# Two mixer sections of a transformer kernel: another order of matmul groups, filter taps and norms

## The reference, cut to what matters

```python
h = rmsnorm(x) ; p = h @ w_in            # 256 x N_IN, split over four branches
y = [rwkv7(p0), stick_breaking(p1), retention(p2), conformer_conv(p3)]
x = x + (sum_i sigmoid(h @ w_gate_i) * (y_i @ w_branch_i)) @ w_out

# rwkv7: state = state*w + (state . -kk) (kk*a)^T + v k^T ; y = state . r    (a scan over tokens)
# stick breaking: z = q k^T of normed q and k ; ls = log_sigmoid(-z)
#                 attn = exp(z + reverse cumulative sum of ls) ; o = attn v
# retention: scores * decay, times v, layernorm per head, times silu(gate)
# conv: u = a * sigmoid(b); 31 causal taps per channel + bias; layernorm; silu
```

## Time and profile before

| | us |
|---|---|
| median of three runs | 1497.53 |
| the profiled execution, own time | 1498.04 |
| its span, first to last instruction | 1496.1 |
| TensorE busy | 1433.5 |
| VectorE busy | 1071.6 |
| ScalarE busy | 857.8 |
| GpSimd busy | 110.7 |
| first mixer, Gram rounds and inverse up to `squares(2)` | 106 to 151 |
| first mixer, rest of the inverse, conv moments, two `apply` | 151 to 208 |
| first mixer, scan | 208 to 272 |
| second mixer, the same three stretches | 609 to 653, 653 to 710, 710 to 775 |

### The profile page before, as it was taken

How to read it: one execution, slowest core, us unless ns; L and a number is a source line. 1 busy time by engine, 2 the same in 40 slices (tenths; PEclk the granted TensorE clock), 3 DMA queues, 4 the chain that set the end, 5 groups by cost and what they waited for, 6 DMA issues and landing times. The chain is left out here.

```text
span 1496.1 us, 25275 instructions
## 1 busy us (share of the span) xinstructions
PE 1433.5 (96%) x10170; PEld 1245.1 (83%) x10170; DVE 1071.6 (72%) x1513; ACT 857.8 (57%) x1220; POOL 110.7 (7%) x130
## 2 busy tenths in 40 slices
PE   8997988999999999889899899999999999999999
PEld 7886978999999999778889777777777778798888
DVE  5885575656555679658557788998889888667764
ACT  4776426444444456743643667777777775447642
POOL 1056000000000001730000000000000000002000
PEclk9998999999999999989999799999999999999999
DMA  8542233355555455313335189999999998543331
GB/s 324 170 142 75 97 113 110 117 178 177 189 190 187 167 163 168 113 58 113 122 105 195 61 292 351 356 366 352 352 352 370 353 352 278 186 155 104 99 128 43
DMA packets 83526, 292.52 MB, mean 196 GB/s; under 512 B 9174, under 2 KB 13126, under 8 KB 83278
## 3 DMA queue, kind: packets, MB, share of 16 engines
q1 hardware_dynamic: 83406, 290.87, 55.6%
HBM read 289.76 MB, written 1.06 MB: 194 GB/s over the span
## 5 line engine op out<-in xcount | busy, mean ns | idle before, releaser
L402 DVE TENSOR_TENSOR ring_lo<-ring,weights_hi 128x1024 fp32r<-128x1024 f32 x345 | 421.4, 1235 | 193.7 <-ACT weights_hi L381 190.9
L381 ACT ACTIVATE weights_hi<-ring 128x1024 fp32r<-128x1024 f32 x345 | 357.2, 1055 | 187.4 <-PE bank_P L276 140.6
L274 PE MATMUL bank_P<-h_hi,weights_hi 128*128 128x256 f32 x1440 | 421.1, 292 | 12.0 <-DVE ring_lo L402 11.7
L276 PE MATMUL bank_P<-h_hi,ring_lo 128*128 128x256 f32 x1440 | 408.2, 283 | 0.0
L275 PE MATMUL bank_P<-h_lo,weights_hi 128*128 128x256 f32 x1440 | 406.9, 283 | 0.0
L274 PEld LDWEIGHTS bank_P<-h_hi,weights_hi 128*128 128x128 f32 x1440 | 273.3, 190 | 21.8 <-DVE ring_lo L402 12.9
L276 PEld LDWEIGHTS bank_P<-h_hi,ring_lo 128*128 128x128 f32 x1440 | 277.8, 193 | 0.0
L275 PEld LDWEIGHTS bank_P<-h_lo,weights_hi 128*128 128x128 f32 x1440 | 273.8, 190 | 2.3 <-issue 1.9
L275 PE MATMUL bank_P<-ring_lo,gathered_hi 128*96 128x512 f32 (+1 forms) x384 | 143.4, 374 | 0.0
L553 POOL TENSOR_TENSOR arena<-arena 128x256 f32<-128x256 f32 x98 | 89.7, 915 | 359.4 <-ACT arena L1068 337.1
L402 DVE TENSOR_TENSOR ring_lo<-ring,tokens_hi 128x1024 fp32r<-128x1024 f32 x76 | 90.3, 1215 | 0.0
(11 more groups left out here) (563 smaller groups left out, 2625.0 us busy)
## 6 DMA issues: line engine op xcount, KB each, us to landing
ring<-stream SPq DMA_DIRECT2D x541, 512.0 KB, 4.5
cst<-consts SPq DMA_DIRECT2D x1, 1520.0 KB, 16.7
arena<-x SPq DMA_DIRECT2D x2, 512.0 KB, 4.9
arena<-bias_vec SPq DMA_DIRECT2D x8, 128.0 KB, 3.1
arena<-params SPq DMA_DIRECT2D x1, 955.5 KB, 5.7
out<-arena SPq DMA_DIRECT2D x3, 256.0 KB, 2.1
arena<-params SPq DMA_DIRECT2D x2, 256.0 KB, 10.5
arena<-bias_vec SPq DMA_DIRECT2D x8, 64.0 KB, 2.7
```

The source lines that it names most:

```text
L274: pe.matmul(out, hi, x_hi, start=start, stop=False, skip_group_check=True)
L276: return pe.matmul(out, lo, x_hi, start=False, stop=stop, skip_group_check=True)
L381: a.activation(self.slots[i % len(self.slots)], env["ring"][:, slot, :], ACT.Copy)\
L402: v.tensor_tensor(env["ring_lo"][:, slot, :], env["ring"][:, slot, :], self.slots[i % len(self.slots)].bitcast(F32), ALU.subtract).then_in ...
```

## The change

The sizes and results of all operations stay. What moves:

- `SCALED` is 6: six slots for scaled taps.
- The scan's stream products go 4, 4, 4 in place of 6, 6: four behind `scan_rhs` (and `sb_z`), four behind `scan_sa` (and `sb_cum`), four behind `scan_state`, before `attend`.
- ScalarE has six taps in each Gram round and not eight (up to 21, 27, 33, 39 and not 23, 31, 39, 47), the others in the inverse (42, 45, 50 at high parts 37, 38 and 39).
- VectorE does its own four taps of a round two and two, around a low part.
- In round 3 VectorE does `M_0` and `TI_0` directly behind `gram_3`; before, two low parts and two norm reciprocals stood between.
- The `sbq` norms and two of the `sbk` norms move into the inverse; `conv_y` goes behind `TI_4`; low parts and reciprocals of the conv and retention layernorms change places.
- In the scan VectorE writes `S_{c+1}` ahead of the softplus; the numbers of high and low parts at each step are new, and the high part of a step stands behind that step's `sb_ln` or `sb_a`.
- The loading of the second block's parameters waits for `conv_out` and not for the key norm.

```diff
-SCALED = 3
+SCALED = 6
@@ tensor, scan
-            gate_products(6)
+            gate_products(4)
             scan_sa(c)
             if c % 2 == 1:
                 sb_cum(hh)
-            gate_products(6)
+            gate_products(4)
             if c < NCH - 1:
                 scan_state(c)
+            gate_products(4)
@@ scalar
-            conv_taps(17 + 8 * cp)
             a.wait_ge(*after(f"p_BK_{cp}"))
             act(BK[...], f"BK_{cp}")
             hi.upto(29 + 2 * cp)
-            conv_taps(21 + 8 * cp)
+            conv_taps(18 + 6 * cp)
             hi.upto(30 + 2 * cp)
+            conv_taps(21 + 6 * cp)
             gate(cp)
-            conv_taps(23 + 8 * cp)
...
-        hi.upto(36)
-        conv_taps(len(CONV))
         m_copy(1)
         hi.upto(37)
+        conv_taps(42)
         m_copy(2)
         hi.upto(38)
+        conv_taps(45)
...
         hi.upto(39)
+        conv_taps(len(CONV))
         m_copy(4)
...
+        hi.upto(45)
         a.wait_ge(*after("conv_lin"))
         act(scr, acc, ACT.Tanh, "conv_th", scale=0.5)
...         in the scan, c even
-                hi.upto(44 + 12 * c // 8)
                 ... sb_ln
+                hi.upto(46 + 3 * hh)
...         c odd
-                hi.upto(44 + (12 * c + 6) // 8)
                 ... sb_a
+                hi.upto(47 + 3 * hh)
@@ vector, Gram rounds
+            if cp == 3:
+                v.wait_ge(*after("p_M_0"))
+                tt(M[:, 0], ..., MUL, "M_0")
+                tt(TI, G[:, :, 0, :], pair_ident, ADD, "TI_0")
+            else:
+                taps(4 * cp, 4 * cp + 2)
             lo.upto(29 + 2 * cp)
             if cp < 3:
-                taps(4 * cp, 4 * cp + 4)
+                taps(4 * cp + 2, 4 * cp + 4)
             lo.upto(30 + 2 * cp)
-            if cp >= 2:
-                sb_norm("sbq", cp - 2)
@@ vector, inverse
         lo.upto(37)
+        sb_norm("sbq", 0)
         mt_copy(2)
...
         lo.upto(38)
+        sb_norm("sbq", 1)
         mt_copy(3)
         inverse_add(2)
+        lo.upto(39)
         sb_norm("sbq", 2)
-        lo.upto(39)
+        sb_norm("sbk", 0)
         inverse_add(3)
         ... ret_xc
         lo.upto(40)
-        ... conv_y
+        sb_norm("sbk", 1)
         inverse_add(4)
         ... rg_silu
+        ... conv_y
         lo.upto(41)
+        reciprocal of ret_std, half 0
         ... conv_xc
-        reciprocal of ret_std, half 0 ; lo.upto(42) ; half 1
-        reciprocal of conv_std ; lo.upto(43)
+        lo.upto(42) ; reciprocal of ret_std, half 1
         ... ret_out
+        lo.upto(43) ; reciprocal of conv_std ; lo.upto(44)
         ... conv_lin
-        lo.upto(44)
-        sb_norm("sbk", 0)
         apply("ret", 1, (P1, P0), range(1))
+        sb_norm("sbk", 2)
+        apply("ret", 1, (P1, P0), range(1, 2))
         ... conv_out
-        apply("ret", 1, (P1, P0), range(1, 4))
-        sb_norm("sbk", 1)
-        sb_norm("sbk", 2)
+        apply("ret", 1, (P1, P0), range(2, 4))
@@ vector, scan
-            lo.upto(44 + (12 * c + 6) // 8)
             ... sa_c
-            softplus, if c is even
-            lo.upto(44 + (12 * c + 12) // 8)
+            lo.upto(45 + 3 * hh + c % 2)
             ... S_{c+1}
+            softplus, if c is even, else lo.upto(47 + 3 * hh)
```

More of the change, by code:

```diff
@@ L1144, in scalar @@
         gate(6)
-        hi.upto(43)
         hi.upto(44)
         gate(7)
+        hi.upto(45)
         a.wait_ge(*after("conv_lin"))
@@ L1164, in scalar @@
                 act(at_, (Z0, Z1)[hh % 2][:, 0:384], ACT.Exp, f"sb_a_{hh}")
+                hi.upto(47 + 3 * hh)
             if c not in (0, 4):
-                q = 8 + (c - 1 if c < 4 else c - 2)
-                hi.upto(44 + 2 * (q - 7))
-                gate(q)
+                gate(8 + (c - 1 if c < 4 else c - 2))
         hi.upto(56)
@@ L1355, in taps @@
                     stt(acc[:, 0, :], u[:, 0, k:k + T], w, acc[:, 0, :], MUL, ADD, "first_taps" if k == DVE_TAPS - 1 else None)
+        pair_ident = C("ident_pair").unsqueeze(1).broadcast_to([P, NCH, HD])
         for cp in range(NCH // 2):
@@ L1361, in vector @@
                C("grams").unsqueeze(1).broadcast_to([P, 2, 4 * HD]), MUL, f"gram_{cp}")
+            if cp == 3:
+                v.wait_ge(*after("p_M_0"))
+                tt(M[:, 0], by_chunk(BX), C("negstrict").unsqueeze(1).broadcast_to([P, NCH, HD]), MUL, "M_0")
+                tt(TI, G[:, :, 0, :], pair_ident, ADD, "TI_0")
+            else:
+                taps(4 * cp, 4 * cp + 2)
             lo.upto(29 + 2 * cp)
             if cp < 3:
-                taps(4 * cp, 4 * cp + 4)
+                taps(4 * cp + 2, 4 * cp + 4)
             lo.upto(30 + 2 * cp)
-            if cp >= 2:
-                sb_norm("sbq", cp - 2)
-        pair_ident = C("ident_pair").unsqueeze(1).broadcast_to([P, NCH, HD])
-        v.wait_ge(*after("p_M_0"))
-        tt(M[:, 0], by_chunk(BX), C("negstrict").unsqueeze(1).broadcast_to([P, NCH, HD]), MUL, "M_0")
         def mt_copy(k):
@@ L1410, in apply @@
                 h_part("m_lo", "m_hi", 3)
-        lo.upto(36)
         ret_s(0)
         ret_s(1)
-        tt(TI, G[:, :, 0, :], pair_ident, ADD, "TI_0")
         mt_copy(1)
         lo.upto(37)
+        sb_norm("sbq", 0)
         mt_copy(2)
@@ L1430, in vector @@
         lo.upto(40)
-        v.wait_ge(*after(f"tap_{len(CONV) - 1}"))
-        for j in range(2):
-            ts(acc[:, j, :], acc[:, j, :], 0.5, R("conv_b", j), MUL, ADD, name="conv_y" if j else None)
+        sb_norm("sbk", 1)
         inverse_add(4)
@@ L1437, in vector @@
         tt(rg, rg, rgt, MUL, "rg_silu")
+        v.wait_ge(*after(f"tap_{len(CONV) - 1}"))
+        for j in range(2):
+            ts(acc[:, j, :], acc[:, j, :], 0.5, R("conv_b", j), MUL, ADD, name="conv_y" if j else None)
         lo.upto(41)
+        v.wait_ge(*after("ret_std"))
+        link(v.reciprocal(rq[:, 0, :], rq[:, 0, :]))
         v.wait_ge(*after("conv_sum"))
@@ L1441, in vector @@
             stt(acc[:, j, :], Z0[:, 0:T], -1.0 / T, acc[:, j, :], MUL, ADD, "conv_xc" if j else None)
[L1442 to L1449, removed]
+        lo.upto(42)
+        link(v.reciprocal(rq[:, 1, :], rq[:, 1, :]))
         for j in range(2):
@@ L1452, in vector @@
         tt(rg, rg, rkk, MUL, "ret_out")
+        lo.upto(43)
+        v.wait_ge(*after("conv_std"))
+        link(v.reciprocal(at_[:, 0:T], at_[:, 0:T]))
+        lo.upto(44)
         for j in range(2):
@@ L1477, in vector @@
                     ts(Se[:, j, :], S[:, c, j, :], dec[:, j, c:c + 1], None, MUL)
-            if c % 2 == 0:
-                z = (Z0, Z1)[hh % 2][:, 0:384]
-                v.wait_ge(*after(f"sb_z_{hh}"))
-            lo.upto(44 + (12 * c + 6) // 8)
             v.wait_ge(*after(f"p_sa_{c}"))
@@ L1499, in vector @@
                         stt(S[:, c + 1, j, :], o, d, Se[:, j, :], MUL, ADD, f"S_{c + 1}" if j else None)
+            if c % 2 == 0:
+                z = (Z0, Z1)[hh % 2][:, 0:384]
+                v.wait_ge(*after(f"sb_z_{hh}"))
+                v.wait_ge(*after(f"sb_ln_{hh}"))
+                stt(az, z, 0.0, exz, MAX, ADD, f"sb_sp_{hh}_raw")
+                for o in (0, T):
+                    tt(az[:, o:o + P], az[:, o:o + P], C("strictT"), MUL, f"sb_sp_{hh}" if o else None)
+            else:
+                lo.upto(47 + 3 * hh)
         lo.upto(56)
@@ L1626, in routing_sync @@
         sp.wait_ge(*after("x_3", "dense"))
-        sp.wait_ge(*after("sbk_n", "mix1"))
+        sp.wait_ge(*after("conv_out", "mix1"))
         sp.dma_start(prm2, env["dram"]["params2"]).then_inc(env["sem"]("params2_in"), 16)
```

## The result

The changed kernel takes 1458.15 us (median of four runs, 1457.30 to 1458.84), the kernel before 1497.55 beside it. The ratio is 0.9737, with a 95% interval of 0.9723 to 0.9751: 39.4 us less, where 38.0 had been worked out.

The account below looks back on a forecast made before the run. TensorE, busy 1433.5 of 1496.1 us, was taken as the bound, so only its waits and low-clock work could be won. 30.8 (Gram rounds) - 0.4 (conv part) + 7.6 (scan) = 38.0 us, giving 1459.5 us; 8-in-10 range 1452 to 1474.

Parts of the forecast that it names:

- The cause of the late gates: Gram rounds: ScalarE stands 3.78 us at a tap for GpSimd, which waited 4.66 us for VectorE's tap 11, delaying high parts.
- the walk: Gram rounds to second squares, dated step by step: all gates in time, least slack 0.8 us, first mixer 44.26 to 28.6.
- What would show it: Signs in the later trace: first squares 16 us earlier, near 129 us; scan waits only at scan_rhs 3, 5, 7.
- The first conv moment: Conv part: conv_y queued behind a reciprocal, TI_4 and rg_silu ends at 179.6, TensorE wants it at 178.29; 1.35 us wait.
- The second moment: Conv part: conv_xc behind a low part and a reciprocal comes at 183.5, so TensorE waits 0.9 us more.
- the third bank fill: Retention products: VectorE has 6.0 us of work before the first retention output, not 4.8; wait 2.3 us, not 1.7.
- that part's sum: Rest of inverse, conv moments, apply: scan starts 0.2 us later in each mixer, 0.4 us lost in both.
- the bounds: Rest of inverse, conv, apply: 2 us gained to 4 us lost in each mixer, including 1.7 for a low-clock gate.
- the third rival: New waits in the conv part bite: each mixer loses 4 us and not 0.2; 1467 us, chance 0.2.
- The scan: Scan waits for S_{c+1}: 3.7 and 3.9 us won, 7.6 in all; 1.0 of each 1.1 stays after chunks 2, 4, 6.
- The second rival: The scan's waits all go, 13.5 us won and not 7.6; 1453.5 us, chance 0.1.
- The slower rival: Low clock holds from the new waits up to the scan: 25 us of TensorE work takes 50; 1509.5 us, chance 0.03.

Follow-up runs that it names:

- Experiment 10: The kernel before with one edit, ScalarE's taps at six in a round, three slots kept; 1475.15 us, ratio 0.9859.
- Experiment 4: The changed kernel with ScalarE's taps at eight in a round, six slots kept; 1469.14 us, ratio 0.9821 to the kernel before.
- 2: The changed kernel with three slots for scaled taps in place of six; 1458.51 us, ratio 0.9741 to the kernel before.
- 9: The changed kernel with conv moments first, retention output first, and high part ahead of Abs, Exp, Ln in chunks 2, 4, 6; 1442.60 us.
- experiment 6: The changed kernel with conv_y back ahead of the key reciprocal and TI_4, conv_xc ahead of ret_std's low part and reciprocal; 1452.60 us.
- experiment 3: The changed kernel with M_0, TI_0 and the two query reciprocals back behind the round's low parts; 1461.44 us, ratio 0.9763.
- 5: The changed kernel with VectorE's low part behind S_{c+1} in chunks 2, 4 and 6; 1453.56 us, ratio 0.9718 to the kernel before.

## Why the prediction was right

**The cause of the late gates** was named rightly: ScalarE standing at taps for GpSimd, handed through ScalarE's queue to the high parts and through VectorE's to `M_0` and `MT_1`. GpSimd was late by its own rate and by waiting for VectorE's tap 11, and the prediction had both. Experiment 10 removes 11.1 of 15.85 us with nothing but the number of taps. Experiment 4, eight taps in the changed kernel, brings back only 4.5; with VectorE's new order tap 11 comes nearly in time there. The six slots, which I had let ScalarE's freedom rest on together with the six taps, have no share (2, at six taps a round).

**The dates** of the walk held. Against the walk's first squares at 129.7, counted from a round that starts at 106.28, they came 23.36 us behind the round's start (walk: 23.4). `M_0` was written 19.1 us behind it (walk: 19.6). The low part of gate 3, the tightest, was written 3.9 us behind it (walk: 3.7), 0.7 us before TensorE began that gate (walk: 0.8). No gate waited. The stretch took 28.41 us (worked out: 28.6). One date under "What would show it" contradicts this walk: the first squares came near 129 us as it says (128.67), but that is 14.8 us earlier than before and not 16; 16 us is near the shift of the second squares (16.8).

**The first conv moment** waits 1.36 us in the first mixer (predicted 1.35) and 1.72 in the second. The chain is the one described: VectorE's low part 40, reciprocal, `TI_4`, `rg_silu`, `conv_y`, and TensorE at the end of it.

```profile
156.55 1.23 DVE L402 TENSOR_TENSOR ring_lo<-ring,weights_hi 128x1024 fp32r<-128x1024 f32 x1 [1.92 <-ACT weights_hi L381]
157.69 1.75 DVE L1327 RECIPROCAL arena<-arena 128x256 f32<-128x256 f32 x1
159.47 1.41 DVE L1206 TENSOR_TENSOR arena<-arena,bank_Y 64x512 f32<-64x512 f32 x2
...
162.10 0.74 DVE L1208 TENSOR_SCALAR arena<-arena,mixer_params 128x256 f32<-128x256 f32 x2
```

The second moment waits 0.57 us (0.9), the third bank fill 2.14 (2.3).

**The term that was off** is that part's sum: +0.2 us predicted in each mixer, +1.23 and +1.59 measured. The sum of the waits was near (4.3 us before and 4.1 after in the first mixer), and the 1.7 us at the low clock behind the third bank fill weren't in the sum; they stood in the bounds and in the third rival only, priced at a gate. The second mixer is 0.4 us worse, as its first conv moment waits 1.72 us. There the kernel before had a low clock as well (5.41 us in the last section), but at no cost: the slow bank fills lasted through the 1.7 us that the first mixer waited behind them, and the stretch took 57.1 us in both mixers.

**The scan** did what was written: no wait at chunks 1, 2, 4 and 6, and three waits of 1.03 us at `scan_rhs` 3, 5 and 7 (predicted 1.0), because the high part stands behind Ln. The second rival, that they all go, would have been the right forecast for two further lines of code (9).

**The total** was closer than its parts deserve, and that is luck: 38.0 us predicted, 36.3 in the changed stretches, and 4.0 more in the profiled execution from code that the change leaves as it is.

**The slower rival** fell: the clock did fall behind the third bank fill's wait, but for part of 12.31 us, at a cost of 1.7 us in each mixer and not 25. The Trainium skill (TensorE: Matmul & The Clock Gate, "HAM oscillation — how this bites in real kernels") tells of a kernel that falls back at every wait. That agrees with the long waits of the Gram rounds here (7.0, 5.5 and 4.2 us before, 3.2 us twice in experiment 10), each with a stretch at the low level begun in it or behind it. It does not hold for shorter ones: 2.74 us without a fall in experiment 6, 2.14 us with one in the change.

## What to carry to other kernels

When an engine waits, follow its queue back to the slowest hand-over and ask for the rate there: eight taps of 1.0 us in a round of 7.5 us held the other engines up, and six didn't. Look also for a circle in which the slow engine itself waits for one that it holds up (tap 11 here). Making one late step early shows the next one behind the same cause (`M_0`, then `MT_1`, 4.9 us won and not 15.85), and more buffers don't help a rate that is already fast enough. Put the copies that only prepare later work (here a high part) ahead of a long chain of activations if their input is ready, not behind it. And before a gain is put down to an edit, look at the clock of the stretch in a kernel that left it alone: here 1.7 us came and went without any edit to it.

## What the runs showed of the hardware that I had not expected

- The clock behind a wait of 2 us or so isn't settled by the wait's length. A wait of 2.15 us in experiment 3, one of 2.13 us in 5 and one of 2.74 us in 6 left it at 1.00; one of 2.14 us at the same place in the changed kernel was followed by 12.31 us at 0.86. In the kernel before, the two mixers differ in the same way: the two bank fills behind a wait of 1.84 us took 3.72 us in the first and 5.41 us at 0.68 in the second.

```profile
692.94:698.35 5.41, 5.40 (x16) 0.68 0.29 97
```

- The same matmuls behind the second scan took 721.9 to 725.6 us in thirteen kernels. Between the kernel before and the changed one the difference of 3 us arises around the routing, where TensorE works in pieces. The rows are the same stretch of 22.5 us behind the second scan, before and then after: granted clock 0.81 before, 0.86 after, and the changed kernel does 103 matmuls in it and not 88. In the 21.5 us behind it the clock is 0.92 and 1.00.

```profile
836.00:858.50 22.50, 19.38 (x88) 0.81 0.11 32
```

```profile
798.80:821.30 22.50, 20.04 (x103) 0.86 0.15 47
```

- GpSimd's taps got longer with the change, 991 ns and not 915 in the mean, since more of them run beside VectorE: of the 98, 44 overlap a low part (36 before, mean 1.2 us), and 4 run while VectorE rests (22 before, 0.73 us). VectorE's two taps beside GpSimd took 1.37 to 1.84 us, against 0.51 each when GpSimd rests.
